# Turning all four merged pieces of a mixer by DMA, with two vector steps moved to ScalarE

## The reference, cut to what matters

```python
for l in range(2):
    x = x + 0.5 * swiglu_ffn(rmsnorm(x), w_ffn1_in[l], w_ffn1_out[l])          # width 2816
    q, k, v, g, p, c, gates = split(rmsnorm(x) @ w_in[l])
    y_ret  = (retention(q, k, v) * silu(g)) @ w_ret_out[l]                     # 4 heads of 128
    y_pool = pool_mixer(p) * pool_scale[l]
    y_conv = silu(layernorm(depthwise_conv_31_taps(glu(c)))) @ w_conv_out[l]   # 512 channels
    gates  = sigmoid(gates + gate_bias[l])
    merged = gates[0] * y_ret + gates[1] * y_pool + gates[2] * y_conv          # 256 x 1024
    x = x + merged @ w_out[l]
    x = x + 0.5 * swiglu_ffn(rmsnorm(x), w_ffn2_in[l], w_ffn2_out[l])
return rmsnorm(x)
```

## Time and profile before

| | |
|---|---|
| median of three executions | 1127.97 us |
| the profiled execution | 1128.66 us |
| its span, first to last instruction | 1126.9 us |
| TensorE busy in the span | 1119.3 us, 99% |
| VectorE busy | 803.1 us, 71% |
| ScalarE busy | 649.7 us, 58% |
| GpSimd busy | 30.6 us, 3% |
| granted TensorE clock, mean | 0.998 |

### The profile page before, as it was taken

How to read it: one execution, slowest core, us unless ns; L and a number is a source line. 1 busy time by engine, 2 the same in 40 slices (tenths; PEclk the granted TensorE clock), 3 DMA queues, 4 the chain that set the end, 5 groups by cost and what they waited for, 6 DMA issues and landing times.

```text
span 1126.9 us, 13064 instructions
## 1 busy us (share of the span) xinstructions
PE 1119.3 (99%) x5006; PEld 926.2 (82%) x5006; DVE 803.1 (71%) x985; ACT 649.7 (58%) x744; POOL 30.6 (3%) x68
## 2 busy tenths in 40 slices
PE   9999999999999999999999999999999999999997
PEld 7888888888888878888888888888888888888886
DVE  6856565899998775655476655478999987665543
ACT  7755545763657675554475554376637476756442
POOL 0100000000100000000000000000001001000000
PEclk9999999999999999999999999999999999999999
DMA  9896666763756787656587656467637677867551
GB/s 357 311 271 209 215 241 192 248 206 118 258 215 192 210 286 208 222 187 224 159 279 261 216 192 229 176 213 251 199 122 266 238 193 224 269 220 224 159 187 38
DMA packets 130862, 244.65 MB, mean 217 GB/s; under 512 B 99040, under 2 KB 100448, under 8 KB 106224
## 3 DMA queue, kind: packets, MB, share of 16 engines
q1 hardware_dynamic: 128016, 236.61, 63.8%
q0 software_dynamic: 1648, 6.06, 1.5%
q10 hardware_dynamic: 1136, 1.15, 0.3%
HBM read 219.16 MB, written 1.05 MB: 195 GB/s over the span
## 4 chain that ended last, share of the span: by engine, by line
PE 97%; DMA 1%; DVE 1%; ACT 0%; SPq 0%; issue 0%; POOLq 0%; POOL 0%; DVEq 0%; ACTq 0%
PE acc L419 31%; PE acc L421 31%; PE acc L420 31%; DMA xT_planes<-x_planes 1%; PE acc L463 1%; PE acc L468 1%; PE acc L472 1%; PE ret L684 0%; PE tr L595 0%; PE tr L604 0%; DMA hT_planes<-h_planes 0%; PE tr L513 0%; DVE xT_lo L1302 0%; DVE hT_whole L1293 0%; DVE w_lo L1248 0%; ACT xT_hi L851 0%
## 5 line engine op out<-in xcount | busy, mean ns | idle before, releaser
L1248 DVE TENSOR_TENSOR w_lo<-raw,w_hi 128x2048 fp32r<-128x2048 f32 (+2 forms) x204 | 445.3, 2213 | 87.0 <-ACT w_hi L817 87.0
L817 ACT CAST w_hi<-raw 128x2048 fp32r<-128x2048 f32 (+2 forms) x204 | 375.1, 1849 | 212.2 <-PE acc L421 206.0
L419 PE MATMUL acc<-w_hi,xT_hi 128*128 128x512 f32 x1152 | 450.8, 391 | 0.6 <-DVE xT_lo L1302 0.6
L421 PE MATMUL acc<-w_hi,xT_lo 128*128 128x512 f32 x1152 | 448.5, 389 | 0.0
L420 PE MATMUL acc<-w_lo,xT_hi 128*128 128x512 f32 x1152 | 448.2, 389 | 0.0
L419 PEld LDWEIGHTS acc<-w_hi,xT_hi 128*128 128x128 f32 x1152 | 216.3, 188 | 45.7 <-DVE xT_lo L1302 1.0
L421 PEld LDWEIGHTS acc<-w_hi,xT_lo 128*128 128x128 f32 x1152 | 216.2, 188 | 45.3
L420 PEld LDWEIGHTS acc<-w_lo,xT_hi 128*128 128x128 f32 x1152 | 216.4, 188 | 44.0
L1331 DVE SCALAR_TENSOR_TENSOR h<-acc,rs,silu_gate 128x256 f32<-128x256 f32 x88 | 42.5, 483 | 148.1 <-ACT silu_gate L884 148.1
L419 PE MATMUL acc<-w_hi,hT_hi 128*128 128x512 f32 x348 | 135.4, 389 | 0.0
L420 PE MATMUL acc<-w_lo,hT_hi 128*128 128x512 f32 x348 | 135.4, 389 | 0.0
(11 more groups left out here) (144 smaller groups left out, 649.7 us busy)
## 6 DMA issues: line engine op xcount, KB each, us to landing
raw<-in_weights SPq DMA_DIRECT2D x192, 1024.0 KB, 5.1
raw<-in_weights SPq DMA_DIRECT2D x20, 256.0 KB, 5.7
raw<-in_weights SPq DMA_DIRECT2D x8, 512.0 KB, 3.4
bias<-in_gate_bias POOLq DMA_DIRECT2D x6, 512.0 KB, 5.5
x<-in_x SPq DMA_DIRECT2D x2, 512.0 KB, 10.7
scale_row<-in_pool_scale POOLq DMA_DIRECT2D x2, 512.0 KB, 5.9
hT_planes<-h_planes SPq DMA_TRANSPOSE x54, 3.1
band<-in_band POOLq DMA_DIRECT2D x1, 768.0 KB, 6.8
```

Source lines behind the costliest of these rows:

```text
L419: nc.tensor.matmul(o, a_hi, b_hi, start=first, stop=False)
L421: return nc.tensor.matmul(o, a_lo, b_hi, start=False, stop=last)
L817: nc.scalar.copy(w_hi[:, hf % HIGHS, 0:n], raw[:, hf % RAWS, 0:n]).then_inc(hi_split, 1)
L1248: nc.vector.tensor_tensor(w_lo[:, hf % RAWS, 0:n], raw[:, hf % RAWS, 0:n], w_hi[:, hf % HIGHS, 0:n].bitcast(F32), ALU.subtract).then_inc(l ...
```

## The change

It has five parts.

1. Piece (0,0) of `merged` is no longer turned on TensorE but by DMA like the other three. TensorE's eight transposes (four in each layer) go. TensorE waits on `merged_front` before `M_OUT`; ScalarE's high part and VectorE's low part of this piece are made in two halves of 128x256.
2. The orders on ScalarE, VectorE and SyncE from `M_CONV` to the seam are rewritten around the four turns; two of the sums x and their splits are moved up, among the merged pieces.
3. The first tap of the convolution goes from VectorE to ScalarE (`first_tap`), and the groups of taps are shifted, so that none is left behind the retention's merge; `turn_y` stands two k-steps earlier.
4. The scaling of retention by heads goes to ScalarE (`scale_ret`, eight 128x128 instructions in each layer); VectorE multiplies with two of 128x512.
5. In a seam the turn of piece (1,1) is issued together with that of (1,0), ahead of one more weight load.

```diff
 # TensorE, mixer
-                in_block(l, M_GATE_CONV, 1, mid={4: lambda: turn_y(l, 0), 5: lambda: turn_y(l, 1)})
+                in_block(l, M_GATE_CONV, 1, mid={2: lambda: turn_y(l, 0), 3: lambda: turn_y(l, 1)})
...
-                wide(l, M_CONV, M_CONV, 1, side, range(4), True, True,
-                     {(0, 1): lambda: turn_merged(l)})
-                wait_tr_taken(pe, ("m", l))
-                wide(l, M_OUT, M_OUT, 0, xT, range(4), True, False)
+                wide(l, M_CONV, M_CONV, 1, side, range(4), True, True)
+                pe.wait_ge(merged_front, l + 1)
+                wide(l, M_OUT, M_OUT, 0, xT, range(4), True, False,
+                     {(0, 1): lambda: pe.wait_ge(merged_lo_ready, moved(l, 0, 0) + 1)})
 # SyncE, behind the load of half hf
                 if hf % HALVES == 2 * FFN2:
+                    turn_merged(hf // HALVES, 0, 0)
                     turn_merged(hf // HALVES, 0, 1)
                     turn_merged(hf // HALVES, 1, 0)
-                if hf % HALVES == 2 * FFN2 + 1:
+                if hf % HALVES == 2 * FFN2 + 2:
                     turn_merged(hf // HALVES, 1, 1)
-                        for ahead, t, c in ((2, 0, 0), (2, 0, 1), (3, 1, 0), (4, 1, 1)):
+                        for ahead, t, c in ((2, 0, 0), (2, 0, 1), (3, 1, 0), (3, 1, 1)):
 # ScalarE
+            def first_tap(l):
+                act.wait_ge(u_whole, l * T + T)
+                act.wait_ge(pad_zero, l + 1)
+                for c in range(CH):
+                    w = PAR_CONV_W + c * TAPS
+                    nc.scalar.activation(y[:, c, :], uT[:, c, 0:S], ACT.Identity,
+                                         bias=par[:, l, PAR_CONV_B + c:PAR_CONV_B + c + 1],
+                                         scale=par[:, l, w:w + 1]).then_inc(conv_step, 1)
+            def scale_ret(l, t):
+                act.wait_ge(head_rs_ready, l + 1)
+                act.wait_ge(u_split, l * T + t + 1)
+                for hd in range(HEADS):
+                    s = slice(hd * P, (hd + 1) * P)
+                    a = nc.scalar.activation(ua[:, t, s], ret[:, t, s], ACT.Copy,
+                                             scale=head_rs[:, t, hd:hd + 1])
+                a.then_inc(ret_scaled, 1)
 # ScalarE, mixer
                 u_out(l, 1)
+                first_tap(l)
...
                 gate_tanh(l, POOLED, 1, 0)
+                scale_ret(l, 0)
+                scale_ret(l, 1)
...
                 gate_tanh(l, CONV, 1, 1)
+                split_merged(l, 0, 0)
                 cast(ahead(M_CONV))
+                split_merged(l, 0, 1)
                 merged_high(l, 0, 0)
-                split_merged(l, 0, 1)
                 split_merged(l, 1, 0)
                 cast(ahead(M_CONV) + 1)
                 merged_high(l, 0, 1)
+                cast(ahead(M_OUT))
                 split_merged(l, 1, 1)
-                cast(ahead(M_OUT))
                 merged_high(l, 1, 0)
+                split_x(l, 3, 0, 0)
                 merged_high(l, 1, 1)
+                split_x(l, 3, 0, 1)
                 seam(l, 3, ahead(M_OUT))
 # VectorE, mixer (conv_taps: 8 -> 10 and 5 -> 3 in two groups, the last four taps gone)
+                merge(l, CONV, 0, 0, merged_all)
                 gate_z(l, CONV, 1, 1)
-                merge(l, CONV, 0, 0, merged_all)
                 sub(l * HALVES + 2 * M_CONV + 3)
                 merge(l, CONV, 0, 1, merged_all)
+                merged_join(l, 0, 0)
                 merged_low(l, 0, 0)
                 merge(l, CONV, 1, 0, merged_all)
+                merged_join(l, 0, 1)
                 sub(l * HALVES + 2 * M_CONV + 4)
-                merge(l, CONV, 1, 1, merged_all)
-                merged_join(l, 0, 1)
                 merged_low(l, 0, 1)
                 sub(l * HALVES + 2 * M_OUT + 3)
                 merged_join(l, 1, 0)
+                merge(l, CONV, 1, 1, merged_all)
+                merged_low(l, 1, 0)
+                add_next(l, 3, 0, 0)
+                add_next(l, 3, 0, 1)
                 merged_join(l, 1, 1)
-                merged_low(l, 1, 0)
                 merged_low(l, 1, 1)
-                seam(l, 3, l * HALVES + 2 * M_OUT + 4, True)
+                seam(l, 3, l * HALVES + 2 * M_OUT + 4)
```

More of the change, by code:

```diff
@@ L302, in trunk @@
         merged_lo_ready = sem("merged_lo_ready")
+        merged_front = sem("merged_front")
         ln_stats_ready = sem("ln_stats_ready")
@@ L514, in transpose4 @@
                 mm.then_inc(tr_full, 1)
-            def turn_merged(l):
-                pe.wait_ge(merged_all, l * 4 + 1)
-                transpose4(("m", l), [merged[:, 0, 0, i * P:(i + 1) * P] for i in range(4)])
             def turn_y(l, t):
@@ L887, in seam @@
             def seam(l, norm, hf):
-                split_x(l, norm, 0, 0)
-                split_x(l, norm, 0, 1)
+                if norm != 3:
+                    split_x(l, norm, 0, 0)
+                    split_x(l, norm, 0, 1)
                 square(l, norm, 0)
@@ L1070, in merged_high @@
             def merged_high(l, t, c):
-                if t == c == 0:
-                    wait_tr_full(act, ("m", l))
-                    m = bank(("m", l))
-                else:
-                    act.wait_ge(merged_joined, moved(l, t, c) + 1)
-                    m = mT_whole[:, c, :]
-                nc.scalar.activation(xT_hi[:, 4 * c:4 * c + 4, tokens(t)],
-                                     m.rearrange("p (k n) -> p k n", k=4),
-                                     ACT.Copy, scale=0.5).then_inc(x_hi_ready, 1)
+                act.wait_ge(merged_joined, moved(l, t, c) + 1)
+                m = mT_whole[:, c, :].rearrange("p (k n) -> p k n", k=4)
+                n = 2 if t == c == 0 else 4
+                for i in range(0, 4, n):
+                    nc.scalar.activation(xT_hi[:, 4 * c + i:4 * c + i + n, tokens(t)],
+                                         m[:, i:i + n, :], ACT.Copy, scale=0.5
+                                         ).then_inc(x_hi_ready, 1)
             def mixer(l):
@@ L1334, in hidden, with seam @@
                                                ).then_inc(taken[t][IN_BANK[g]], 1)
-            def seam(l, norm, hf, own=False):
-                add_next(l, norm, 0, 0)
-                add_next(l, norm, 0, 1)
-                if own:
+            def seam(l, norm, hf):
+                if norm == 3:
                     sub(hf)
+                else:
+                    add_next(l, norm, 0, 0)
+                    add_next(l, norm, 0, 1)
                 x_join(l, norm, 0, 0)
@@ L1533, in retained @@
             def retained(l, t):
[L1534 to L1540 removed]
+                dve.wait_ge(ret_scaled, l * T + t + 1)
+                nc.vector.tensor_tensor(ua[:, t, :], ua[:, t, :], g_silu[:, t, :], ALU.mult
+                                        ).then_inc(ret_ready, 1)
             def merge_first(l, t, n):
@@ L1575, in merged_low @@
             def merged_low(l, t, c):
-                m = bank(("m", l)) if t == c == 0 else mT_whole[:, c, :]
-                s = (slice(None), slice(4 * c, 4 * c + 4), tokens(t))
-                x_high_count[0] += 1
-                dve.wait_ge(x_hi_ready, x_high_count[0])
-                nc.vector.scalar_tensor_tensor(
-                    xT_lo[s], m.rearrange("p (k n) -> p k n", k=4), 0.5,
-                    xT_hi[s].bitcast(F32), ALU.mult, ALU.subtract
-                ).then_inc(tr_taken[TURN[("m", l)] % 2] if t == c == 0 else merged_lo_ready, 1)
+                m = mT_whole[:, c, :].rearrange("p (k n) -> p k n", k=4)
+                n = 2 if t == c == 0 else 4
+                for i in range(0, 4, n):
+                    s = (slice(None), slice(4 * c + i, 4 * c + i + n), tokens(t))
+                    x_high_count[0] += 1
+                    dve.wait_ge(x_hi_ready, x_high_count[0])
+                    a = nc.vector.scalar_tensor_tensor(
+                        xT_lo[s], m[:, i:i + n, :], 0.5, xT_hi[s].bitcast(F32),
+                        ALU.mult, ALU.subtract)
+                    a.then_inc(merged_front if n == 2 and i == 0 else merged_lo_ready, 1)
             def ln_stat(l, t):
```

47 lines of the change are left out of this document (16 added, 31 removed).

## The result

| | before | after |
|---|---|---|
| median of six executions | 1128.16 us | 1139.20 us |
| lowest and highest | 1127.56 to 1128.73 | 1136.21 to 1141.91 |
| the profiled execution | 1128.66 us | 1139.13 us |
| its span | 1126.9 us | 1137.3 us |

The ratio of the medians is 1.0094, with a 95% interval of 1.0083 to 1.0104: 11 us slower than the kernel before. Forecast were 7.0 us more, 1135.0 us, and a range that ended at 1138.5. The direction was right, the size was not, and the changed kernel's executions also lie 5.7 us apart where those of the kernel before lie 1.2 us apart.

The account below looks back on a forecast made before the run. TensorE, busy 99% at full clock, was taken as the bound. Front and seam delays of 3.1 us in layer 0 and 3.9 us in layer 1 made 7.0 us, added to 1127.97 for 1135.0 us; range 1128.8 to 1138.5.

Parts of the forecast that it names:

- What bounds the kernel: Whole kernel: TensorE is busy 99% of the span at full clock, so anything that makes it wait is paid in full.
- What the change can win: Removed turn 0.50 us in each layer plus layer 0's seam wait 0.78 us: 1.8 us together, too little to show.
- The front piece's way: Piece (0,0) before M_OUT: split, DMA of 3.24 us and join make VectorE wait 1.4 us and TensorE idle 0.78 us.
- What is late next: M_OUT's second chunk: a low part and a weight subtraction come late, leaving TensorE 1.6 us behind before.
- into the seam: Seam after M_OUT: x's first join 3.9 us late in layer 0; TensorE ends 3.1 us later there, 3.9 in layer 1.
- the turn is hidden: Rival at the front: slack in VectorE's and ScalarE's lists absorbs the waits; 1126.2 us, not slower; chance 0.10.
- the lag dies in M_OUT: Rival: the 1.6 us lag at the critical subtraction is caught up within M_OUT; 1130.4 or 1128.6 us; chance 0.12.
- turns are slower in company: Rival: DMA turns take longer, as with a weight load ahead of one (8.0 us); over 1138.5 us; chance 0.10.
- Parts at no cost: First tap, scaling by heads, shifted taps and turn_y, and the seam's moved issue: nothing; the tap at most 0.5 us.
- Scaling by heads: Retention's scaling on ScalarE: eight instructions, 2.2 to 3.3 us, covered by slack, so no cost in time.

Follow-up runs that it names:

- the denser order: Kernel before with parts 1, 2 and 5, last conv gate's tanh after piece (0,0)'s split, ScalarE's and VectorE's front lists reordered: 1131.84 us, ratio 1.0027.
- the changed kernel with u's turn early: The changed kernel with u's first turn issued ahead of the weight load that stood before it: 1139.98 us, ratio 1.0106.
- the tanh behind the split: Kernel before with parts 1 and 2, ScalarE's tanh of the last conv gate moved behind the split of piece (0,0): 1134.21 us, ratio 1.0051.

## Why the prediction was wrong, and where it was right

**What bounds the kernel**: right. TensorE is busy 99% in both, and the time follows TensorE's idle in every run but one, where the clock fell too. **What the change can win**: right. The turn went, and part 5 took the seam's idle of layer 0 away (parts 3 to 5, part 5); neither shows in a time beyond its interval.

**The front piece's way**: right in mechanism and place, a little dear. The new wait of VectorE was 1.17 us for 1.4, the idle before `M_OUT` 0.52 us in steps for 0.78, since the turn took 3.09 us for 3.24 and the tanh ahead of the split took 0.53 us from start to start for 0.63. **What is late next** and **into the seam**: right. The second chunk idles 0.31 and 0.71 us in steps (0.4 and 0.8 forecast), and the passages are 2.70 and 3.44 us longer (3.1 and 3.9). The last low part of layer 0's seam ends at 399.96 + 1.14 = 401.1, or 400.5 with `M_CONV`'s shift of 0.6 us taken off; forecast was 400.9. So the term of 7.0 us measures 6.1 in this change; part of that came of the order of the lists, as the denser order shows. Of the forecast's rivals, "the turn is hidden" and "the lag dies in M_OUT" fell with the row at 370.36 and the 3.44 us of layer 1, which has nothing that could give it back. The third, "turns are slower in company", is the one whose number came out (over 1138.5), but not by its way: the front's turn took 3.09 us, less than the 3.24 taken, and the slow turn was one of u, which neither forecast nor rival had looked at. That the measured time lies in its range is luck.

The Trainium skill, VectorE: DVE Perf Modes, "The three transpose paths", has 1309 ns for a tile by DMA; from the end of the split to the join the trace has 3.09 us for eight tiles. Its rule to keep to TensorE where PSUM will do is borne out by this case: 0.5 us of TensorE were exchanged for a way of 3 us.

**Parts at no cost** is the step that failed, in the sentences on the first tap: "Four instructions of about 0.4 us", and "nothing, or 0.1 us; if the cover is gone up to 0.5". It costs 4.1 us in this change. Three things were wrong in it.

First, the duration. I took a tap on ScalarE from the forms nearest by size. The groups of the changed kernel, by line and form, have 590 ns and a step of (2.08 - 0.59) / 3 = 0.50 us:

```profile
L984 ACT ACTIVATE y<-uT,par 128x256 f32<-128x256 f32 x8 | 4.2, 590 | 0.1
```

The tap reads both its scale and its bias from a tile, one number for each partition (`par`); the nearest row, 418 ns, names no such tile. The Trainium skill, ScalarE: Activation LUTs, "What ACT_TABLE_LOAD costs", would have given this size: 186 ns and 0.833 ns for each column, 93 ns more for each such operand, 93 ns of overlap between neighbours, so an estimate of 585 ns for one and 2.06 us for four. The trace agrees, with 590 ns and 2.08 us. I had read the rows by size and not by operands.

Second, the way of the lag. I had VectorE 0.7 us late up to the decay and the decay ending 0.1 us before TensorE wanted it. With the tap's right size that is 0.7 + 0.5 = 1.2 us, and TensorE idles: 0.54 us in steps in the row of 266.23 and 0.2 at the next scores; 0.83 came in by the landmarks. So layer 0, where the turns landed as before, is this term mis-sized, and the "up to 0.5" was nearly its end.

Third and largest, layer 1 was taken to be like layer 0 because the one profile of before showed it so. There u's turns took 9.4 us, with VectorE waiting 0.31 us for them. In the changed kernel's profile they took 12.6. Without the tap turns as late cost TensorE 1.1 us (after without part 3); with it 3.3. Had they taken 9.4 us again, the table makes it an estimate of 0.1 us, so for the landing of that one profile the term was right. The forecast looked at what the tap adds to a list and not at what it adds to a chain that starts with a DMA whose landing varies: copy, tap on ScalarE, tap on VectorE now follow each other, where before the copy released VectorE at once. The scatter of 5.7 us would fit this, since each late turn is now paid in full, but it is not shown: there is one profile for each kernel, and part 3 alone scatters by 1.4 us only. The clock may have a share in it. The slowest of the six executions, 1141.91 us, had a mean granted clock of 0.996, the other five 0.998 to 1.0, and the changed kernel with u's turn early shows what a short fall of the clock costs; but the 1141.91 us have no trace that could show it.

Why the turn lands late is **open**. It was late in profiles with and without part 3, and in one with parts 1 and 2 only changed by the tanh, so no part owns it. Nor is it a matter of turns alone: in most of the profiles with late turns a weight load just ahead of them was late too. ScalarE's casts between 762 and 772 us waited for a load for 0.41 us in the changed kernel, twice 1.43 us without part 3 and 1.61 and 1.83 us with the tanh behind the split, and not at all in the kernel before, with part 4 and with parts 1 and 2 (nor with parts 4 and 5, at 11.0 us). The 12.6 us are of one execution for each kernel, and other executions of the changed kernel, with times 5.7 us apart, may have had other landings.

**Scaling by heads**, forecast at 2.2 to 3.3 us on ScalarE and nothing for the end: 2.15 us for eight, and no difference that can be measured (part 4 alone). What was missed is its worth to part 3: without it the late VectorE also delays retention's merges, 0.74 us in each layer.

## What to carry to other kernels

Before a step is moved to another engine, look at the duration by its operands and not only its shape, and ask where it stands in a chain that begins with a DMA: an engine that is 58% busy is no cover for a step that a third engine waits for. One profile shows one landing of each transfer; slack that depends on it should be tested with the largest landing that any transfer of its kind shows (8.0 us for x's turns), not with the one that happened. And a handover to DMA is priced from the end of the split to the join, 3 us here, with the lists of both engines walked until a wait takes it up.

## What the runs showed of the hardware that was not expected

There are stretches in which hardly anything moves while a transposing transfer is under way. Busy share of the DMA engines in tenths and GB/s, changed kernel, 770.7 to 774.0 us, in 40 slices, while the first turn of u was under way and ScalarE waited for it:

```profile
DMA  7999999990000002000200020020002000200020
GB/s 177 189 186 168 137 115 84 56 12 0 0 0 0 0 0 99 0 0 0 99 0 0 0 99 0 0 99 0 0 0 99 0 0 0 99 0 0 0 99 0
```

For 2.6 us there is one slice of traffic every 0.3 us, and nothing else; the DMA engines are idle between, so they were not crowded. That is most of the 3.2 us by which this turn was later than before. In the kernel before, in the stretch of the same turn (762.8 to 769.3), the rate is at or under 50 GB/s for at most two neighbouring slices of 0.16 us. What holds it was not found.

A wait of TensorE also costs about 0.1 us at the matmul behind the first one (362.61 stands 0.33 us behind 362.28, where the step is 0.227). The idles of layer 0's front add up to 2.9 us in steps, which less the removed 0.5 and 0.8 us makes 1.6, where the passage is 2.7 us longer. In this passage the changed kernel has ten steps of 0.30 to 0.34 us, the kernel before two; eight more make 0.8 of the difference.

The length of an idle alone does not say whether the clock falls. It stayed at 2.4 GHz (granted 1.00) behind idles of 3.16 us (the changed kernel) and 3.12 us (part 3 alone), and fell to 1.2 GHz (granted 0.50) for 3.4 us behind one of 2.10 us at the same matmul (the changed kernel with u's turn early).
